# Keys, queries and the MLP's first matrix in 512-column products, a reordered second block, and 17 weight slots for the experts

## The chip, the cores and the metric

One core of one Trainium2 chip runs the whole program. The metric is the device time of one execution in microseconds (us). The core has TensorE (PE, with its weight loads, PEld, shown apart), VectorE (DVE), ScalarE (ACT), GpSimd (POOL) and SyncE (SP), which issues nearly all weight transfers. PSUM has eight banks of 128 x 512 float32.

## The reference, cut to what matters

Two layers of a first block, then one second block, on 256 tokens of width 1024, all in float32:

```
for l in (0, 1):
    x = x + rms(mixers(rms(x) @ w_in[l]) @ w_mix_out[l])           # NSA, retention, RWKV, conv
    q = rms(x) @ wq ; k, v = split(rms(mem) @ wkv)                  # cross attention, 4 heads of 256
    x = x + rms(softmax(q k^T / 16) v @ wo)
    x = x + rms(square(relu(rms(x) @ w1)) @ w2)                     # w1: 1024 x 4096
h = rms(x)                                                          # second block
x = x + groupnorm([attention, lru, convolution](h @ w_in_2)) @ w_out_2
x = x + sum over the 2 chosen of 32 experts of gate * (silu(h @ gate_e) * (h @ up_e)) @ down_e
```

## The kernel before, in words

The weights lie in DRAM as one stream of units of 128 x 2048 float32 (1 MiB each; `pieces` gives their order, `pack_weights` fills it). SP loads them in order (`load`, L2800) into ring slots; each load waits until its slot is free. Outside the experts and the convolution's taps, every unit is split in two float32r parts: ACT copies it rounded (`upper`, "hi"), DVE subtracts ("lo", L204, 128x2048). Both run LOOK = 2 units ahead, in `unit()`, which each engine's program calls once per unit; a split waits for PE to finish the unit three before. A product of two split operands is three products, high by high, high by low and low by high (`mm3`).

`proj` (L619) makes two 128 x 256 outputs of a unit: for each output eight k-steps of three 256-column products, 48 in all, into one bank. MLP: `up(g)` is two such units (L1040), `down(g)` two units of 24 products of 512 columns, 48 in all; PE runs up(g+1), then down(g). The accumulators of down hold four banks. ACT evicts up's result with Relu, DVE squares, ACT and DVE split it again. Keys and queries are eight `proj` units per layer with one ACT copy each.

`fill` spreads the units of the gates over the mixers' small products. In the retention and RWKV part of each layer ACT waits for `rsq`, takes the inverse root ("rvar"), and then does two fills; DVE does a fill after `aP`, another after `rout`, the lower part of oT1, then the masked matrices that PE's U, T and `within(3)` products wait for.

Second block: PE's program (from L1135) runs projections (bq, bk, cvl, cgt, vv, zx, xg), four tap units (float32 products with raw weights), log-space sums, and 26 filler products (`warm`, ones by constants) in three places; then three group norms and `tok_out(axv, "bout")`, which begins when all three norms are in both parts.

Experts (`few`, the path that these inputs take): six units each, four for gate and up, two for down, never split. There are SLOTS = 15 slots: 4 ring, 2 in ht, 6 in hl, 3 in the arena. Those 15 are loaded before the branch on the flag; after it every load waits for the unit that held its slot. Per expert PE does gate_up (2 x 16 products of 128x512, two 64-column tiles side by side), turn, place, scatter(e-1), gather, down (16). All of X stays in SBUF; four banks collect the expert outputs; at the end DVE adds them to X in four steps and ACT's queue stores two halves. A scatter is four float32 products with 64 rows.

## Time and profile before

| | |
|---|---|
| median of 3 runs | 1917.17 us (1914.98 to 1918.26) |
| the profiled execution | 1916.08 us, its span 1914.3 us, mean granted clock 0.994 |
| PE busy | 1850.7 us, 97% |
| DVE, ACT busy | 939.1 us (49%), 767.8 us (40%) |
| chain that ended last | 85% PE, 7% DVE, 3% ACT, 2% DMA |

A row of the timeline has its start, its length, engine, line, operation, tiles, shapes and count, and in brackets how long the engine sat idle before it and who ended that. A row of a windows table has the busy time of each engine in the stretch, the granted clock (1.00 is 2.4 GHz, 0.50 is 1.2 GHz), the DMA engines' share and GB/s.

### The profile page before, as it was taken

To read this page: it belongs to the slowest core of one execution; us is meant where nothing else is said; L and a number is where in the kernel's file an instruction comes from. 1 tells how busy PE (TensorE), PEld (TensorE's weight loads), DVE (VectorE), ACT (ScalarE), POOL (GpSimd) and SP (SyncE) were. 2 spreads that over 40 slices of the span, in tenths; PEclk is the share of its full clock that TensorE was granted. 3 is DMA by queue.
4 is the path that set the end of the run, shared out by engine and by line. 5 is a ranking of instruction groups with operands and counts; after the bars stand their busy time and mean duration, and the time that the engine had idled before them with its cause. 6 is when DMAs were issued, how large, how long until landed. Compare 5 with 4: busy or idle time off the path is not lost.

```text
span 1914.3 us, 28059 instructions
## 1 busy us (share of the span) xinstructions
PE 1850.7 (97%) x12114; PEld 1467.8 (77%) x12114; DVE 939.1 (49%) x1135; ACT 767.8 (40%) x1078; POOL 72.8 (4%) x90
## 2 busy tenths in 40 slices
PE   7998999999999999899999999999999999999998
PEld 6998998988999899899898899988874444444332
DVE  4866638646555686653864655575751111110001
ACT  4653344555444465334455544446532111111111
POOL 0000014000000000001400000000000000000000
PEclk9999999999999999999999999999999999999999
DMA  8434365534555533436553555543457999999996
GB/s 314 149 123 159 111 254 203 201 129 160 193 183 191 189 134 118 156 112 256 201 203 127 183 184 193 181 165 111 169 209 300 422 421 421 421 421 421 421 421 280
DMA packets 64512, 440.68 MB, mean 230 GB/s; under 512 B 7372, under 2 KB 7372, under 8 KB 14720
## 3 DMA queue, kind: packets, MB, share of 16 engines
q1 hardware_dynamic: 55296, 399.63, 54.4%
q0 software_dynamic: 8096, 35.30, 5.0%
q10 hardware_dynamic: 992, 3.90, 0.5%
q8 instruction: 97, 1.59, 0.3%
q14 instruction: 31, 0.25, 0.0%
HBM read 428.58 MB, written 10.23 MB: 229 GB/s over the span
## 4 chain that ended last, share of the span: by engine, by line
PE 85%; DVE 7%; ACT 3%; DMA 2%; POOL 2%; issue 1%; DVEq 0%; ACTq 0%; POOLq 0%
PE psum L190 83%; PE psum L194 2%; DVE arena L204 2%; DVE hl L204 2%; DVE arena L214 2%; POOL arena L204 1%; DMA ring<-W 1%; ACT arena L200 1%; ACT L200 1%; DMA cst<-CS 1%; ACT hl L200 0%; DVE ht L204 0%; ACT arena L201 0%; DVE arena L224 0%; DVE arena L227 0%
## 5 line engine op out<-in xcount | busy, mean ns | idle before, releaser
L190 PE MATMUL psum<-ht,hl 128*128 128x256 f32 x4992 | 622.5, 286 | 7.8 <-DVE ht L204 6.4
L190 PEld LDWEIGHTS psum<-ht,hl 128*128 128x128 f32 x4992 | 607.8, 193 | 18.6 <-DVE ht L204 7.7
L204 DVE TENSOR_TENSOR hl<-ring,hl 128x2048 fp32r<-128x2048 f32 (+1 forms) x188 | 428.7, 2286 | 308.9 <-ACT hl L200 308.5
L200 ACT ACTIVATE hl<-ring 128x2048 fp32r<-128x2048 f32 (+1 forms) x188 | 353.3, 1884 | 111.9 <-PE psum L190 102.4
L200 ACT ACTIVATE arena<-psum 128x512 f32<-128x512 f32 (+4 forms) x260 | 132.2, 509 | 391.9 <-PE psum L190 355.9
L190 PE MATMUL psum<-hl,ax 128*128 128x512 f32 x1056 | 243.7, 390 | 0.0
L190 PEld LDWEIGHTS psum<-hl,ax 128*128 128x128 f32 x1056 | 197.3, 188 | 40.2
L190 PE MATMUL psum<-arena 128*128 128x128 f32 (+8 forms) x1520 | 167.9, 290 | 9.9 <-DVE arena L204 7.4
L190 PEld LDWEIGHTS psum<-arena 128*128 128x128 f32 (+3 forms) x1520 | 152.8, 177 | 21.6 <-DVE arena L204 8.0
L204 DVE TENSOR_TENSOR hx_raw<-hx_raw,psum 64x512 f32<-64x512 f32 x32 | 22.1, 691 | 226.1 <-ACT hx_raw L200 226.1
L190 PE MATMUL psum<-hl,ht 128*128 128x512 f32 (+2 forms) x624 | 124.0, 358 | 1.1 <-DVE ht L214 1.1
L190 PEld LDWEIGHTS psum<-hl,ht 128*128 128x128 f32 x624 | 103.4, 189 | 19.5 <-DVE ht L214 1.9
L204 DVE TENSOR_TENSOR arena<-arena 128x512 f32<-128x512 f32 (+9 forms) x128 | 85.8, 670 | 42.2 <-ACT arena L200 36.0
L221 DVE COPY par<-psum 128x256 f32<-128x256 f32 x32 | 13.6, 424 | 185.2 <-PE psum L194 185.2
L190 PE MATMUL psum<-ax,hl 128*128 128x256 f32 x768 | 94.1, 284 | 0.0
L190 PEld LDWEIGHTS psum<-ax,hl 128*128 128x128 f32 x768 | 92.8, 192 | 1.1 <-issue 1.0
L190 PE MATMUL psum<-hl_raw,ax_raw 128*64 128x512 f32 x400 | 90.7, 596 | 0.0
L190 PE MATMUL psum<-cst 128*128 128x256 f32 x272 | 66.2, 401 | 15.7 <-DMA cst<-CS 12.5
L190 PE MATMUL psum<-ring,ax_raw 128*64 128x512 f32 x272 | 72.3, 595 | 0.8 <-DMA ring<-W 0.8
L190 PEld LDWEIGHTS psum<-cst 128*128 128x128 f32 x272 | 54.3, 203 | 23.5 <-DMA cst<-CS 12.5
L190 PE MATMUL psum<-hl_raw,par 128*64 128x512 f32 x224 | 72.1, 593 | 0.0
L201 ACT ACTIVATE arena<-psum 128x2 f32<-128x2 f32 (+1 forms) x56 | 19.9, 355 | 130.1 <-PE psum L190 129.3
(110 smaller groups left out, 1509.1 us busy)
## 6 DMA issues: line engine op xcount, KB each, us to landing
ring<-W SPq DMA_DIRECT2D x238, 1024.0 KB, 4.9
hl_raw<-W SPq DMA_DIRECT2D x78, 1024.0 KB, 17.8
arena<-W SPq DMA_DIRECT2D x36, 1024.0 KB, 17.1
ht_raw<-W SPq DMA_DIRECT2D x26, 1024.0 KB, 16.3
gate_d<-arena POOLq DMA_DIRECT2D x32, 256.0 KB, 3.9
arena<-gate_d POOLq DMA_DIRECT2D x8, 1024.0 KB, 8.9
gn<-GB POOLq DMA_DIRECT2D x10, 512.0 KB, 4.4
arena<-GB POOLq DMA_DIRECT2D x6, 512.0 KB, 5.1
```

The lines of the kernel that those rows point to most:

```text
L190: return Nothing() if self.e is None else self.e.matmul(o, a, b, start=start, stop=stop, skip_group_check=skip_group_check)
L194: return Nothing() if self.e is None else self.e.transpose(o, a, ident)
L200: return self.e.activation(o, a, f, bias=bias, scale=scale)
L201: return self.e.activation(o, a, f, bias=bias, scale=scale, accum_out=accum_out)
L204: return Nothing() if self.e is None else self.e.tensor_tensor(o, a, b, op)
L214: return Nothing() if self.e is None else self.e.scalar_tensor_tensor(out=o, in0=a, scalar=s, in1=b, op0=op0, op1=op1)
L221: return Nothing() if self.e is None else self.e.tensor_copy(o, a)
```

## The change

Four things, in one diff:

1. `proj_two` for keys, queries and up: high and low part of the activations stand behind each other as one 512-column operand under the high weights; the low weights meet the high part in a 256-column product. Two products per k-step, one bank per output (two per unit). ACT copies the second half of the bank, DVE adds the first (`met`).
2. Retention: ACT splits one unit before it waits for `rsq`, and DVE splits it before `aP`; DVE's fill and oT1's lower part move behind the masked matrices.
3. Second block: another order of units and of the three engines' steps; `xg` near the end with the group norm of attention between its halves; the first half of w_out starts when that norm alone is there; 6 fillers for 26.
4. Experts: X goes into the four accumulator banks by an identity product (in place of 9 fillers), its memory and that of `hf` become slots 16 and 17, loaded right behind the branch; the scatter takes high and low part of the output in one 128-row float32r product (ACT makes the high part, DVE the low); the last turn lies inside down(30); the results are copied out by ACT and DVE and stored from two queues.

```diff
+            def proj_two(rhs, *name):
+                u, wh, wl = unit()
+                both = (ht if rhs is hTv else ax)[:, :].rearrange("p (s k t) -> p k s t", s=2, k=8)
+                for q in range(2):
+                    b = bank(*name, q)
+                    cs = slice(128 * q, 128 * q + 128)
+                    for k in range(8):
+                        pe.matmul(psum[:, b, :], wh[:, k, cs], both[:, k, :, :], k == 0, False)
+                        ins = pe.matmul(psum[:, b, 0:256], wl[:, k, cs], both[:, k, 0, :], False, k == 7)
+                    ins.then_inc(s_pe, P(*name, q))
...
-                        pe.wait_ge(s_act, A["qx", 3, l])
+                        pe.wait_ge(s_dve, V["qx", 3, l])
...
                 fill()
+                unit()
                 ac.wait_ge(s_dve, V["rsq", l])
                 inverse_root(L.rrb, "eps5", 1.0 / 64, "rvar", l)
-                fill(2)
+                fill(begun=True)
+                fill()
...
+                def part(dst, *name):
+                    for q in range(2):
+                        ac.wait_ge(s_pe, P[(*name, q)])
+                        act(dst[:, q, :], half(banks[(*name, q)], 1), ACT.Copy, *name, "part", q, after=False)
...
+                def met(dst, *name):
+                    for q in range(2):
+                        ve.wait_ge(s_act, A[(*name, "part", q)])
+                        tt(dst[:, q, :], half(banks[(*name, q)], 0), dst[:, q, :], ADD, *name, after=False)
+                        gone(*name, q)
...
-                        tt(L.sq, L.rl, L.rl, MUL, "sq", g, i, l)
+                        met(L.rl, "up", g, i, l)
+                        stt(L.sq, L.rl, 0.0, L.rl, MAX, MUL, "sq", g, i, l)
...
-                fill()
-                ve.wait_ge(s_act, A["oT1", l])
-                lower(oT[1], L.rcen, "oT", 1, l)
+                fill(begun=True)
...
+            weighted(3)
+            proj(hTv, "xg", between=lambda: group_norm(0, 4, b2.zq[:, 0:4, :]))
...
-            warm(4)
-            group_norm(2, 2, ct1)
-            warm(10)
-            pe.wait_ge(s_dve, V["ynorm", 0])
+            warm(6)
...
+            for j in range(2):
+                u, _, _ = unit()
+                pe.wait_ge(s_dve, V["ynorm", 0])
+                for t in range(2):
+                    out_part(u, j, 0, t)
+                P.mark("unit", u)
+                if j == 0:
+                    group_norm(2, 2, ct1)
+                    group_norm(1, 2, b2.rec[3])
...
-            warm(9)
+            for t in range(2):
+                for j in range(2):
+                    b = bank("xacc", t, j, keep=True)
+                    ins = pe.matmul(psum[:, b, :], C("ident"), Xv[:, t, 512 * j:512 * j + 512], True, False, True)
...
-                            js = slice(64 * j, 64 * j + 64)
-                            ins = pe.matmul(psum[:, 2 * t + j, :], mo.SE[e % 3][js, t, :], mo.YE[e % 2][js, :], e == 0, e == 31)
+                            ins = pe.matmul(psum[:, banks["xacc", t, j], :], mo.SE[e % 3][:, t, :],
+                                            mo.YE[e % 2][:, 512 * j:512 * j + 512], False, e == 31, True)
...
+                elif m == 15:
+                    sp.wait_ge(s_pe, P["xacc"])
+                    sp.wait_ge(s_act, A["hf", 1])
+                elif m == 16:
+                    sp.wait_ge(s_pe, P["logits"])
```

On DVE the second block's last steps now run: attention's norm and its lower part, the recurrence, the convolution's output, the gelu product, then two `unit()` (two splits), the norms of group 2 and group 1.

## Rows read from the trace of the kernel before

**Rows 1.** The page: busy share of PE, and DMA share in 40 slices.
```profile
PE 1850.7 (97%) x12114; PEld 1467.8 (77%) x12114; DVE 939.1 (49%) x1135; ACT 767.8 (40%) x1078; POOL 72.8 (4%) x90
DMA  8434365534555533436553555543457999999996
```
**Rows 2.** Timeline of layer 0's MLP: down, up, down on PE; ACT evicts.
```profile
504.00 11.07 PE L190 MATMUL psum<-hl,ax 128*128 128x512 f32 x48
514.90 11.68 PE L190 MATMUL psum<-ht,hl 128*128 128x256 f32 x96
520.86 0.60 ACT L200 ACTIVATE arena<-psum 128x512 f32<-128x512 f32 x1 [3.78 <-PE psum L190]
526.42 3.82 PE L190 MATMUL psum<-hl,ax 128*128 128x512 f32 x16
```
**Rows 3.** Timeline behind the last query unit of layer 0, PE.
```profile
388.94 7.17 PE L190 MATMUL psum<-arena 128*128 128x256 f32 x32 [0.69 <-ACT arena L200]
```
**Rows 4.** Timeline of layer 0's retention and RWKV part.
```profile
137.95 3.70 ACT L200 ACTIVATE hl<-ring 128x2048 fp32r<-128x2048 f32 x2
139.88 2.29 DVE L204 TENSOR_TENSOR hl<-ring,hl 128x2048 fp32r<-128x2048 f32 x1 [5.15 <-ACT hl L200]
...
152.73 2.28 DVE L204 TENSOR_TENSOR hl<-ring,hl 128x2048 fp32r<-128x2048 f32 x1
158.11 2.08 PE L190 MATMUL psum<-arena 64*128 64x128 f32 x16 [3.64 <-DVE arena L204]
160.12 7.43 PE L190 MATMUL psum<-ht,hl 128*128 128x256 f32 x48
```
**Rows 5.** Windows: PE, PEld, DVE, ACT, POOL busy (count), PEclk, DMA share, GB/s.
```profile
158.00:160.00 2.00, 1.89 (x16) 1.78 (x16) 1.83 (x4) 0.00 (x0) 0.00 (x0) 0.50 0.57 242
```
**Rows 6.** Timeline of the second block before the experts.
```profile
1329.04 3.79 PE L190 MATMUL psum<-arena,cst 128*128 128x256 f32 x24 [3.23 <-DVE arena L214]
...
1383.08 5.34 PE L190 MATMUL psum<-cst 128*128 128x256 f32 x24
...
1389.26 1.75 DVE L227 RECIPROCAL arena<-arena 128x256 f32<-128x256 f32 x1
...
1395.08 1.58 PE L190 MATMUL psum<-arena,cst 128*128 128x256 f32 x4 [2.07 <-DVE arena L204]
1396.45 5.74 PE L190 MATMUL psum<-cst 128*128 128x256 f32 x20
...
1401.84 22.14 PE L190 MATMUL psum<-hl,ax 128*128 128x512 f32 x96
```
**Rows 7.** Windows of the expert stage: its start, its body, the last transfers.
```profile
1440.00:1453.00 13.00, 12.57 (x69) 9.36 (x70) 3.19 (x10) 2.82 (x7) 0.00 (x0) 0.87 0.03 10
1460.00:1880.00 420.00, 419.97 (x2102) 169.84 (x2100) 41.36 (x83) 69.18 (x175) 0.00 (x0) 1.00 1.01 421
1894.00:1900.00 6.00, 5.19 (x28) 2.44 (x28) 1.11 (x2) 1.28 (x2) 0.00 (x0) 1.00 0.30 126
```
**Rows 8.** The chain that ended last, in order of time: two experts' starts.
```profile
1473.89 13.62 PE psum L190 x66
...
1488.28 13.62 PE psum L190 x66
```
**Rows 9.** Timeline: a scatter inside the stage, and the end of the kernel.
```profile
1488.32 1.99 PE L190 MATMUL psum<-gn,arena 64*128 64x512 f32 x8
...
1894.92 0.69 DVE L204 TENSOR_TENSOR hx_raw<-hx_raw,psum 64x512 f32<-64x512 f32 x1 [6.19 <-ACT hx_raw L200]
...
1900.88 3.65 PE L190 MATMUL psum<-hl_raw,par 128*64 128x512 f32 x16
...
1904.58 0.69 ACT L200 ACTIVATE gn<-psum,arena 128x512 f32<-128x512 f32 x1 [5.92 <-PE psum L190]
1905.32 1.99 PE L190 MATMUL psum<-gn,arena 64*128 64x512 f32 x8 [0.79 <-ACT gn L200]
1906.49 2.48 DVE L204 TENSOR_TENSOR resid<-resid,psum 128x512 f32<-128x512 f32 x4 [6.86 <-PE psum L190]
```

More of the change, by code:

```diff
@@ L1186, in tensor @@
             ins.then_inc(s_pe, P("cpw"))
-            warm(4)
-            group_norm(2, 2, ct1)
-            warm(10)
-            pe.wait_ge(s_dve, V["ynorm", 0])
+            warm(6)
+            for t in range(2):
+                for j in range(2):
+                    bank("bout", t, j, keep=True)
+            for j in range(2):
[3 more added lines that the diff above has]
+                    out_part(u, j, 0, t)
+                P.mark("unit", u)
+                if j == 0:
+                    group_norm(2, 2, ct1)
+                    group_norm(1, 2, b2.rec[3])
+            two = [unit()[0] for _ in range(2)]
             pe.wait_ge(s_dve, V["ynorm", 1])
             pe.wait_ge(s_dve, V["ynorm", 2])
-            tok_out(axv, "bout")
+            for t in range(2):
+                for j in range(2):
+                    out_part(two[j], j, 1, t)
+                    if t:
+                        P.mark("unit", two[j])
+                    turn.give(banks["bout", t, j])
             P.mark("b2 end")
@@ L1316, in few @@
                         gather(g, i, shared)
-                    if e < 31:
-                        gate_up(e + 1, 1)
+                    gate_up(e + 1, 1)
                     if g < 8:
                         pe.wait_ge(s_act, A["x", g, i])
-                    down(e)
+                    down(e, between=last if e == 30 else None)
+                down(31)
+                scatter(30)
                 scatter(31)
             def many():
+                for t in range(2):
+                    for j in range(2):
+                        turn.give(banks["xacc", t, j])
                 def expert_in(e):
@@ L1670, in scalar @@
                     unit()
-                    ac.wait_ge(s_pe, P["qx", g, l])
-                    copy(L.qx[:, 2 * g:2 * g + 2, :], half(banks["qx", g, l]), "qx", g, l)
-                    gone("qx", g, l)
+                    part(L.qx[:, 2 * g:2 * g + 2, :], "qx", g, l)
                 for t in range(2):
@@ L1819, in scalar @@
             unit()
+            unit()
+            weights(0)
+            weights(1)
             ac.wait_ge(s_pe, P["zx"])
@@ L1822, in scalar @@
             gone("zx")
-            ac.wait_ge(s_dve, V["sm0"])
-            act(sm[:, :, 1:2], sm[:, :, 0:1], ACT.Exp, "lam exp")
-            act(sm[:, :, 2:3], sm[:, :, 1:2], ACT.Ln, "lam", bias=C("ones")[:, 0:1])
-            weights(0)
-            weights(1)
-            unit()
-            ac.wait_ge(s_pe, P["xg"])
-            copy(b2.xg, half(banks["xg",]), "xg")
-            gone("xg")
+            unit()
+            take_ya(0)
+            take_ya(1)
+            keeps(3)
+            unit()
+            weights(2)
             for nm, dst, o in (("wa", t1, 0), ("wx", t2, 2)):
@@ L1855, in scalar @@
             gone("cu")
-            group_root(1, 2, aL)
-            take_ya(3)
+            unit()
+            weights(3)
+            ac.wait_ge(s_dve, V["loga"])
+            act(aL, t1, ACT.Exp, "aL")
             ac.wait_ge(s_pe, P["cvar"])
@@ L1860, in scalar @@
             gone("cvar")
-            group_root(0, 4, b2.zq[:, 4:6, :])
-            group_cut(1, 2)
+            take_ya(2)
+            take_ya(3)
+            act(t3, t1, ACT.Tanh, "t3")
             ac.wait_ge(s_dve, V["cnorm"])
             act(ct1, cu, ACT.Tanh, "csilu", scale=0.5)
+            group_root(0, 4, b2.zq[:, 4:6, :])
+            ac.wait_ge(s_dve, V["uvar"])
+            act(t1, t1, ACT.Sqrt, "ustd", scale=-1.0)
+            ac.wait_ge(s_pe, P["xg"])
+            copy(b2.xg, half(banks["xg",]), "xg")
+            gone("xg")
             group_cut(0, 4)
+            ac.wait_ge(s_dve, V["gelu"])
+            act(t3, t3, ACT.Tanh, "gelu", scale=math.sqrt(2.0 / math.pi))
+            unit()
+            unit()
             group_root(2, 2, ct2)
+            group_root(1, 2, aL)
             group_cut(2, 2)
-            for _ in range(3):
+            group_cut(1, 2)
+            for _ in range(2):
                 unit()
@@ L2264, in vector @@
                     masked(1, i)
+                fill()
+                ve.wait_ge(s_act, A["oT1", l])
+                lower(oT[1], L.rcen, "oT", 1, l)
                 fill()
@@ L2649, in few @@
             def few():
-                shared = 6
                 def prep(g):
```

339 lines of the change are left out of this document (201 added, 138 removed).

## The prediction

> **What bounds the kernel now.** I read the page first. PE is busy for 97% of the span and the DMA engines reach nine tenths only in the last quarter [rows 1]. So up to about 1440 us the time is PE's, and a step there is worth what it takes from PE, or from a wait of PE. Then I read PE's timeline in three places. In the MLP products follow each other without a gap [rows 2]. In the retention part PE waits for DVE [rows 4], and the granted clock falls to 0.50 (1.2 GHz) behind that wait [rows 5]. In the second block fillers and waits alternate [rows 6]. The windows and the chain give the expert stage: PE takes 14.39 us per expert [rows 8], while 421 GB/s bring an expert's six units of 1.049 MB in 14.95 us [rows 7]. PE is the faster of the two and lives on the 15 stocked units; the stock runs out just at the end. The transfers stood still from 1440 to about 1453 [rows 7], because all slots were full.
>
> **The change part by part.** The sum is made against the profiled execution, 1916.08 us (span 1914.3 and 1.8 around it), 1.1 us under the median of 1917.17.
>
> *512-column products.* 96 products of 256 columns take 526.42 - 514.90 = 11.52 us, 120.0 ns each; 48 of 512 columns take 514.90 - 504.00 = 10.90 us, 227.1 ns each [rows 2]. A k-step is 3 x 120.0 = 360.0 ns now and 227.1 + 120.0 = 347.1 ns then, 12.9 ns less. There are 48 units (per layer 4 keys, 4 queries, 16 up) of 16 k-steps, 768: 9.9 us. No row shows the split operand (two stretches of 256 columns) or the alternation of widths. If weight loads cost the 120 ns, a k-step could stay at 360 (gain 0) or, if the 256-column product shrinks behind a long one to 227.1/2 = 113.6 ns, save 19.3 ns (14.8 us). I take 9.9, since both terms are measured in this stage.
>
> The Trainium skill (TensorE: Matmul & The Clock Gate, Back-to-back issue gap) puts a warm product at its columns over 2.4 GHz plus 2.5 ns; by it the fixed part that a k-step saves would be 2.5 ns and the whole 1.9 us in place of 9.9. The rows disagree with it: 120.0 and 227.1 ns leave over 13 ns per product, so the sum stays with the rows.
>
> The new work lies beside PE. ACT copies two halves instead of one bank (0.60 us for 512 columns [rows 2]) and DVE gains two additions of 256 columns per unit, under 0.69 us each (a 512-wide step on half the partitions, [rows 9]). With split (2.29), square and lower part that is under 5.1 us on DVE per up unit, against 5.5 us of PE and another 10.9 us of down for every two. Banks: up now takes two of the four that down leaves, and gets a bank back after two units; the eviction ends about 3.2 us behind the unit and PE asks 5.5 us behind it. Without that cover each late bank would cost its lateness 32 times. In front of the scores PE now waits for ACT and DVE in turn instead of ACT alone (idle 0.69 us [rows 3]): +0.3 us per layer, +0.6. Sum of this part: -9.3; bounds +1 and -14.
>
> *Retention.* PE sat 3.64 us before 158.11 waiting for a bank that DVE frees with its second T step [rows 4]; three more waits before it make 6.7 us, and at 0.50 the next 48 products took 7.43 us in place of 6.0. DVE's queue in between holds three splits of 2.29, and the first waited for ACT, which came to it only at 137.95 behind the inverse root. The change puts that split before `aP`, so the masked matrices start about 4 us earlier. But they are followed by both remaining splits, and the second of these now waits for ACT, which makes its high part only behind oT1's lower part. By hand: masked matrices end at 145.4, split 147.7, oT1 148.4, ACT's copy 150.3, split 152.7, T steps 155.6, against 158.1. That is 2.5 us per layer and 5.0 for two; the clock still falls. Bounds: 0, and 9 per layer if the waits and the slow clock all go. I take 5.0.
>
> *Second block.* From 1268.07 (its first product) to 1401.84 PE spends 133.8 us. In it are 26 fillers, 12 of them in 5.34 us and the last ten in 5.74, 12.9 in all, and five waits, the first 3.23, the last 2.07, together 8.8 [rows 6]. Work: 112.1 us. The new order has six fillers (2.7 us). Placing the three engines' steps I find three waits, for `cu` (1.1), `cusq` (1.7) and the square of attention's output (2.2): 5.0. The first half of w_out (48 products, 10.9 us) then ends at 1268.1 + 112.1 + 2.7 + 5.0 + 10.9 = 1398.8. The second half needs the other two norms. On DVE they stand behind the recurrence and the gelu product (ends about 1392.7), then two splits (4.6), and for each norm a reciprocal of 1.75 [rows 6], two products of 0.5, a wait for ACT's rounding and a lower part of 0.69: about 1405.6. So PE waits near 6 us and the clock falls as it does in rows 5, worth 2.5. End: 1405.6 + 10.9 + 2.5 = 1419.0, against 1401.84 + 22.14 = 1424.0. Gain 5.0; bounds -16 (no wait) and +3 (two waits more of this size). The SP loads behind these units keep their distance to the end of w_out, so the stage behind it only moves.
>
> *Experts.* The stock grows from 15 to 17 units. Both loads fit in the 13 us in which nothing moved, and their slots are empty by then; so 175 units instead of 177 come after 1453, at 1.049 MB / 421 GB/s = 2.49 us each: -5.0. The scatter falls from 1.99 us [rows 9] to four products of 227 ns, so PE would need 13.4 us per expert; being still faster than the transfers, it gains nothing. The identity products (four float32 ones of 512 columns, about 3.4 us) take the place of nine fillers (4.0): 0. DVE's two extra steps per expert (0.69 each, ACT first) end under 3 us behind down, beside gate_up's 3.65. The tail: the last units land near 1898.5 [rows 7]; now down(31) starts at 1900.88, since turn(31), scatter(30) and its weights come in turn [rows 9]. In the new order turn(31) is done by then, and down starts as its weights land: -2.4. Behind it the output needs two ACT and one late DVE step (1.9 in place of 0.69), scatter 0.9 for 2.0, copies on two engines 1.2 for 2.5, hence about -1.2 more, and scatter(30), 0.9, lies now in the cover of the former: together -2.7. Sum -7.7; bounds -3 and -12.
>
> Sum: -9.3 - 5.0 - 5.0 - 7.7 = -27.0; 1916.1 - 27.0 = 1889.1, or 1890.2 by the median. I predict 1890.
>
> **The rivals.**
> *A k-step that stays at 360 ns.* For it: 256-column products are 13 ns over their columns, and nobody knows whether that is the load of weights. Against: the 512-column ones are over by the same. The gain is then 27.0 - 9.9 = 17.1: 1900.
> *The second block without its last wait.* For it: my DVE time is a hand schedule, and a split or two may have run earlier. Against: the order in the diff puts both before the norms. Another -8: 1882.
> *The experts turn from DMA to PE (slower).* PE now waits for transfers 1.6 us per expert once the stock is used up, by my numbers from about expert 18 on. Waits of 2 to 4 us were followed by 0.50 in rows 5 and behind 1395.08 [rows 6]. If that happens here, 13.4 us of work become up to 26.8 against 14.95 of supply. PE decides below a mean clock of 13.4 / 14.95 = 0.90. At 0.75 an expert costs 17.9, 2.9 more, 14 times 41 us: 1931. Against it: single waits would be under 1.4 us, and a late PE finds its stock full and has no waits. [...] No row of this stage shows a clock below 1.00 between 1460 and 1880 [rows 7], but there PE had no waits.
> *The change doesn't do what it says:* the two slots are loaded too late to be of use and the banks of up make PE wait. Then only retention, block and tail remain, about 1905.
>
> **How the numbers follow.** Forecast, all four terms near their values (1884 to 1896): 0.55. K-step at 360: 0.12. No last wait: 0.17. Late slots or banks: 0.09. PE-bound experts: 0.04. Other: 0.03. The range leaves out the slow rival, 1905 and a little below 1882: 1879 to 1902. The likeliest is 1890. About 0.2% (4 us) is what a measurement here can tell from no change. Faster by more: 0.94; within: 0.02; slower: 0.04.
>
> **What would show it.** MLP: 96 products of up (now 64) in about 11.1 us instead of 11.52, and no idle PE before them. Retention: the wait before `within(3)` at 155 to 156 less the earlier shift. Second block: a wait of about 6 us before the last 48 products of w_out, the end of w_out 5 us nearer to the block's first product. Experts: 421 GB/s throughout, two loads within 2 us of the branch, PE idle 1.6 us per expert in the last third, the last transfer 5 us nearer to the branch. The prediction is wrong if PE waits for banks in up, if the clock in the last third is under 0.9, or if transfers pause after 1455.

## The result and the profile after

The changed kernel takes 1896.53 us (median; 1893.93 to 1898.58) against 1917.72 (1914.98 to 1918.53): a ratio of 0.9889, 95% interval 0.9875 to 0.9903, that is 21.2 us less. I had predicted 1890.0, 27.0 less, with a range of 1879 to 1902. The profiled execution took 1893.93 us with a span of 1892.0, 22.3 less than before. The direction and three of the four terms came out near their values; the largest term came out at a third.

The page of the changed kernel: busy time, then the DMA engines' share and GB/s in 40 slices.

```profile
PE 1805.5 (95%) x11168; PEld 1416.6 (75%) x11168; DVE 1020.0 (54%) x1293; ACT 795.9 (42%) x1157; POOL 72.9 (4%) x90
DMA  8444365534555434336553455442458999999997
```

PE is busy for 95% of the span where it was 97% [rows 1], with 946 records of products fewer, and DVE has 81 us more to do.

To see where the time went I used DVE's 188 splits (128x2048) as milestones, since the n-th split is the same step in each kernel, outside the retention part and the second block. Each column is the length of a stretch of the run: start to split 13; retention and RWKV of layer 0 (to split 21); from there to the MLP (split 57: the gates, output product, keys, queries); MLP (93); the same of layer 1 with its retention (109, 145, 181); the second block to the branch (PE's 12 fillers behind it); branch to the first gate product on DVE; from there to the 32nd; the tail. The first line has us in the changed kernel's profile, each other line what a profile has more or less than that.

```
               start  ret.0  keys0   MLP0  ret.1  keys1   MLP1  block branch experts  tail    sum
changed       100.19  68.69 288.11 202.99 137.56 277.63 214.70 137.29  15.94  431.00 17.94 1892.04
before         -0.03  +2.96  -0.51  +1.76  +2.67  +0.64  +1.46  +4.31  +1.43   +6.11 +1.43  +22.25
predicted              +2.5   +1.4   +3.3   +2.5   +1.4   +3.3   +5.0     (  +5.0  ) +2.7   +27.0
```

The lines of after that answer to [rows 2] and [rows 3]: PE in layer 0's MLP (down, up, down) and the start of the scores.

```profile
478.73 11.11 PE L191 MATMUL psum<-hl,ax 128*128 128x512 f32 x48
489.68 11.45 PE L191 MATMUL psum<-ht,hl 128*128 128x512 f32 x64
500.96 11.11 PE L191 MATMUL psum<-hl,ax 128*128 128x512 f32 x48
...
386.52 1.78 PE L191 MATMUL psum<-arena 128*128 128x256 f32 x7 [0.93 <-DVE arena L205]
```

The 64 products of up follow each other without idle time (so no wait for banks in up, as predicted) and take 500.96 - 489.68 = 11.28 us, where 96 took 11.52. That is 352.5 ns for a k-step: a gain of 7.5 ns, not 12.9. Down takes 10.95 where it took 10.90.

The keys of layer 0, with DVE's step that held them up:

```profile
333.40 0.69 DVE L205 TENSOR_TENSOR arena<-psum,arena 128x512 f32<-128x512 f32 x1 [2.03 <-DMA arena<-GB]
...
337.36 5.80 PE L191 MATMUL psum<-ax,hl 128*128 128x512 f32 x32
344.67 5.89 PE L191 MATMUL psum<-ax,hl 128*128 128x512 f32 x32 [1.51 <-DVE resid L215]
```

Between two key units stands a wait that the kernel before didn't have: there the 96 products of these two units are one piece.

```profile
340.28 11.68 PE L190 MATMUL psum<-ax,hl 128*128 128x256 f32 x96
```

The second unit now takes two banks, and its banks were those of the mixers' output, which DVE gave back only after it had added them to X. DVE had itself stood for 2.03 us for a gain vector. In layer 1 the same wait is 0.50. From the first key product to the first of the scores it is 49.16 us in layer 0 (386.52 - 337.36) and 48.16 in layer 1; before, it was 48.66 in both (388.94 - 340.28 in layer 0). So in keys and queries one layer lost half a us and the other gained it.

Retention, layer 0, after ([rows 4, 5] before): PE, DVE, ACT, then the window behind the wait.

```profile
156.07 2.08 PE L191 MATMUL psum<-arena 64*128 64x128 f32 x16 [5.07 <-DVE arena L205]
158.08 6.54 PE L191 MATMUL psum<-ht,hl 128*128 128x256 f32 x48
...
150.68 2.29 DVE L205 TENSOR_TENSOR hl<-ring,hl 128x2048 fp32r<-128x2048 f32 x1 [1.98 <-ACT hl L201]
153.07 0.69 DVE L205 TENSOR_TENSOR arena<-psum,cst 128x512 f32<-128x512 f32 x1
...
155.32 0.69 DVE L205 TENSOR_TENSOR arena<-psum,cst 128x512 f32<-128x512 f32 x1
...
148.73 1.91 ACT L201 ACTIVATE hl<-ring 128x2048 fp32r<-128x2048 f32 x1 [7.46 <-DVE ax L205]
...
156.00:158.00 2.00, 1.93 (x16) 1.79 (x16) 1.83 (x4) 0.00 (x0) 0.00 (x0) 0.50 0.54 225
158.00:160.00 2.00, 2.00 (x13) 1.92 (x12) 1.83 (x4) 0.00 (x0) 0.00 (x0) 0.68 0.00 0
```

within(3) starts at 156.07 where it started at 158.11: my hand schedule said 155.6. Its wait is now one of 5.07 in place of four that came to 6.7, and it ends with DVE's second T step, which stands behind a split, which stands behind ACT, which sat 7.46 us waiting for oT1's lower part.

Second block, after ([rows 6] before): PE, then DVE.

```profile
1383.65 1.89 PE L191 MATMUL psum<-arena,cst 128*128 128x256 f32 x8
1385.20 5.83 PE L191 MATMUL psum<-hl,ax 128*128 128x512 f32 x24
1397.27 13.24 PE L191 MATMUL psum<-hl,ax 128*128 128x512 f32 x48 [6.24 <-DVE ax L205]
...
1384.13 4.49 DVE L205 TENSOR_TENSOR hl<-ring,hl 128x2048 fp32r<-128x2048 f32 x2
1388.72 1.75 DVE L228 RECIPROCAL arena<-arena 128x256 f32<-128x256 f32 x1
...
1392.94 1.75 DVE L228 RECIPROCAL arena<-arena 128x256 f32<-128x256 f32 x1
```

The wait of 6 us before the last 48 products is there (6.24), and they take 13.24 us instead of 10.9, 2.3 more. From the block's first product (1259.11) to the last of w_out (1410.5) it is 151.4 us; predicted 150.9, before 155.9.

Experts: windows of their first and last part, PE's first wait for weights, then pieces of the chain that ended last, with the tail at its end ([rows 7, 8, 9] before).

```profile
1460.00:1660.00 200.00, 199.47 (x1020) 87.39 (x1019) 44.96 (x76) 47.67 (x106) 0.00 (x0) 1.00 1.01 421
1680.00:1860.00 180.00, 161.33 (x798) 69.79 (x798) 34.94 (x57) 37.20 (x82) 0.00 (x0) 1.00 1.01 421
...
1655.08 0.61 PE L191 MATMUL psum<-resid,ax_raw 128*64 128x512 f32 x1 [0.54 <-DMA arena<-W]
...
1472.50 12.54 PE psum L191 x62
...
1485.80 12.54 PE psum L191 x62
...
1626.94 27.93 DMA arena<-W
...
1879.11 3.67 PE psum L191 x16
1883.52 0.74 DVE rounded L215
```

PE needs 13.30 us per expert (1485.80 - 1472.50), the transfers run at 421 GB/s throughout, and the chain changes from PE to DMA with the transfer that starts at 1626.94. PE first waits for weights at 1655.08, before the first product of the 18th expert. Between 1680 and 1860 PE is idle for 18.7 of 180 us, 1.6 per expert, and the clock stays at 1.00.

### The profile page after: what moved, and what is told of

Same layout as the page of the kernel before. It is cut to its first block, busy times and chain, and to the rows that moved or that the text cites. A ratio compares the mean times of both kernels' runs of the same rounds, so it can differ in the third digit from the quotient of the medians.

```text
span 1892.0 us, 26308 instructions
## 1 busy us (share of the span) xinstructions
PE 1805.5 (95%) x11168; PEld 1416.6 (75%) x11168; DVE 1020.0 (54%) x1293; ACT 795.9 (42%) x1157; POOL 72.9 (4%) x90
## 4 chain that ended last, share of the span: by engine, by line
PE 73%; DMA 13%; DVE 8%; ACT 3%; POOL 2%; issue 1%; DVEq 0%; ACTq 0%; POOLq 0%
PE psum L191 71%; DMA hl_raw<-W 5%; DMA arena<-W 3%; DVE arena L205 2%; PE psum L195 2%; DVE hl L205 2%; DMA resid<-W 2%; DMA ring<-W 2%; DVE arena L215 2%; POOL arena L205 1%; DMA ht_raw<-W 1%; ACT arena L201 1%; ACT hl L201 1%; ACT L201 1%; DMA cst<-CS 1%
## 5 line engine op out<-in xcount | busy, mean ns | idle before, releaser
L191 PE MATMUL psum<-ht,hl 128*128 128x256 f32 (+1 forms) x4352 | 616.3, 302 | 7.1 <-DVE ht L205 6.6
L191 PEld LDWEIGHTS psum<-ht,hl 128*128 128x128 f32 x4352 | 570.7, 191 | 46.8 <-DVE ht L205 8.0
L201 ACT ACTIVATE arena<-psum 128x256 f32<-128x256 f32 (+5 forms) x278 | 128.9, 466 | 373.4 <-PE psum L191 339.8
L215 DVE SCALAR_TENSOR_TENSOR rounded<-psum,arena,rounded 64x512 fp32r<-64x512 f32 x64 | 48.0, 750 | 94.9 <-ACT rounded L201 93.9
L191 PE MATMUL psum<-ax,hl 128*128 128x256 f32 (+1 forms) x640 | 93.2, 306 | 2.0 <-DVE resid L215 2.0
L205 DVE TENSOR_TENSOR arena<-psum,arena 128x256 f32<-128x256 f32 (+2 forms) x141 | 66.6, 490 | 40.8 <-ACT arena L201 29.2
L191 PE MATMUL psum<-arena,ax_raw 128*64 128x512 f32 x240 | 80.0, 597 | 5.3 <-DMA arena<-W 2.6
L191 PE MATMUL psum<-ring,ax_raw 128*64 128x512 f32 x240 | 79.9, 596 | 5.3 <-DMA ring<-W 2.6
L201 ACT ACTIVATE rounded<-psum,arena 64x512 fp32r<-64x512 f32 x64 | 43.7, 682 | 97.3 <-PE psum L191 96.5
L191 PE MATMUL psum<-rounded 128*128 128x256 f32 (+2 forms) x448 | 76.0, 315 | 1.2 <-DVE rounded L215 1.2
```

Source lines behind the costliest of these rows:

```text
L191: return Nothing() if self.e is None else self.e.matmul(o, a, b, start=start, stop=stop, skip_group_check=skip_group_check)
L201: return self.e.activation(o, a, f, bias=bias, scale=scale)
L205: return Nothing() if self.e is None else self.e.tensor_tensor(o, a, b, op)
L215: return Nothing() if self.e is None else self.e.scalar_tensor_tensor(out=o, in0=a, scalar=s, in1=b, op0=op0, op1=op1)
```

## Experiments

Each kernel was timed beside the kernel before on the same chip. The four a kernels shared one chip, b1, b2, b3 and b5 another, and b4 and the c kernels a third.

```
                         median us (lowest to highest)   ratio to before, 95% interval
a1 narrow products       1901.17 (1899.40 to 1908.24)    0.9914 (0.9894 to 0.9934)
a2 old retention         1899.65 (1898.84 to 1902.63)    0.9897 (0.9879 to 0.9914)
a3 old second block      1903.87 (1902.36 to 1909.51)    0.9917 (0.9901 to 0.9933)
a4 15 slots              1900.80 (1899.00 to 1906.67)    0.9900 (0.9882 to 0.9919)
b1 wide, then narrow     1894.67 (1892.61 to 1902.70)    0.9876 (0.9858 to 0.9895)
b2 cut by norm           1892.51 (1890.28 to 1895.10)    0.9867 (0.9846 to 0.9888)
b3 T steps first         1887.79 (1884.75 to 1888.98)    0.9839 (0.9819 to 0.9858)
b5 banks given earlier   1899.26 (1893.75 to 1904.04)    0.9912 (0.9885 to 0.9939)
c0 changed kernel        1896.90 (1894.45 to 1898.17)    0.9883 (0.9862 to 0.9904)
b4 more work for PE      1923.39 (1919.83 to 1925.80)    1.0026 (1.0015 to 1.0037)
c1 four edits            1876.24 (1875.28 to 1880.03)    0.9782 (0.9763 to 0.9802)
c2 and fillers           1872.37 (1871.42 to 1880.91)    0.9778 (0.9752 to 0.9803)
```

Intervals of 0.4% are as wide as most single terms, so a term is read from the same stretches of the profiles (more or less than the changed kernel's):

```
               start  ret.0  keys0   MLP0  ret.1  keys1   MLP1  block branch experts  tail    sum
c0             -0.01  +1.34  -0.17  -0.46  +1.01  +1.15  +0.04  +0.09  -0.01   +1.08 +0.18   +4.24
a1             +0.13  +0.48  -0.50  +1.56  -0.20  +0.53  +1.46  +0.95  +0.00   -0.38 +0.01   +4.04
a2             +2.44  +2.09  -0.12  -0.05  +1.74  -0.37  -0.02  -0.01  -0.01   -0.10 +0.38   +5.97
a3             +8.56  +0.10  -0.16  -0.01  +0.10  -0.07  +0.00  +5.48  +1.63   -0.15 +0.18  +15.67
a4             +6.00  +1.30  -0.20  -0.02  +0.83  -0.08  +0.06  +0.93  -0.01   +3.95 -0.02  +12.74
b1             +8.05  +0.32  +0.29  -1.38  +0.66  +0.17  -1.33  +1.01  +1.41   -0.32 -0.01   +8.86
b2             +0.01  +0.23  -0.39  -0.46  +0.49  +0.00  +0.00  -2.08  +1.68   +0.67 -0.03   +0.11
b3             +2.19  -5.72  -0.29  -0.05  -6.06  +1.41  -0.11  +0.90  +1.66   +1.10 +0.02   -4.95
b5             -0.01  +0.37  -1.73  -0.01  +0.98  +0.51  +0.02  +0.80  +0.00   -0.98 -0.03   -0.09
b4             +0.16  +0.46  -0.06  -0.05  +0.31  +0.00  +0.02  +0.90  +1.66  +24.99 +1.78  +30.17
c1             -0.16  -5.72  -0.10  -1.39  -6.08  -0.89  -1.48  -1.70  +0.01   -0.13 +0.19  -17.46
c2             -0.06  -5.73  -2.18  -1.39  -6.09  -0.89  -1.49  -4.70  +0.00   +0.67 -0.04  -21.89
```

c0 is the changed kernel once more, and its line is the yardstick: an MLP repeats to 0.5 us, but a stretch with a wait of several us in it only to 1 or 1.3, since the slow clock behind the wait is not equally long each time. The window that was at 0.68 above is at 0.50 in c0, and the 48 products in it took 7.86 us instead of 6.54:

```profile
158.00:160.00 2.00, 2.00 (x11) 1.91 (x10) 1.83 (x4) 0.00 (x0) 0.00 (x0) 0.50 0.00 0
```

The start varies by up to 8.6 us from one execution to the next, whatever the kernel, so single spans are no measure of an edit here. Some other stretches can be judged in the profiles whose kernels have the same steps there. With the retention's order of the change (nine profiles) they average 0.5 us more than the first line in each layer; the block with the new order (nine) reaches up to 1.0 more; the expert stretch with 17 slots and this PE work (eleven) runs from 0.98 less to 1.10 more.

**a1: keys, queries and up in 256-column products.**

```diff
-                        proj_two(hTv, "up", g, i, l)
+                        proj(hTv, "up", g, i, l)
...
-                part(L.rl, "up", g, i, l)
+                act(L.rl, half(banks["up", g, i, l]), ACT.Relu, "up", g, i, l)
```

> The changed kernel (1896.5 us) with keys, queries and up back in 256-column products (three per k-step, one bank per unit, one copy by ACT); all else as changed. My sum gave this part 9.3 us (k-step 360.0 to 347.1 ns, less 0.6 for two waits): 1905.8. The rival reads the trace of the changed kernel: its k-steps in up take 352.8 ns and those of keys and queries between 346.6 and 353, and 2 us of new waits for banks stand among the keys (1.51 of them in layer 0); 16 x 8 x 2 + 8 x 16 k-steps per layer give 3.3 us, less 2.6 of waits in all: 4.0, so 1900.5. If the products don't matter at all it stays at 1896.5. The second block and the expert stage keep their lengths in all three.

Measured 0.9914 against 0.9889 and 0.9883 of the changed kernel, and in the profile 1.56 - 0.50 + 0.53 + 1.46 = 3.05 us more in keys and MLPs. The ratio says more than that, 4.8 to 5.9 us, but 1.6 of it isn't in the products: in all six runs of a1 the time is 3.3 to 3.7 us over the span of its instructions, in every other kernel's runs 1.7 to 2.0. Why is open. The pairs bring 3 us in the MLPs and nothing in the keys and queries: from the first key product to the scores a1 takes 48.65 us in each layer, the changed kernel 49.16 and 48.16. My 9.3 is refuted; the rival (4.0) is near.

**a2: the old order of the retention part.**

```diff
                 fill()
-                unit()
                 ac.wait_ge(s_dve, V["rsq", l])
                 inverse_root(L.rrb, "eps5", 1.0 / 64, "rvar", l)
-                fill(begun=True)
-                fill()
+                fill(2)
```

> The changed kernel with the retention part's old order on ACT and DVE (split behind aP, lower part of oT1 ahead of the masked matrices). My sum gave this order 2.5 us per layer, 5.0 in all: 1901.5, with the wait before within(3) about 1.4 us shorter than the 5.07 of the changed kernel and within(3) 2.5 us later. The rival: the trace shows 2.04 us at within(3) and 2.93 behind the fill after it (a fill at full clock gains 0.9 more), so 5.9: 1902.4. If what is gained there is lost again at the next wait of the same layer, the time stays near 1896.5 and the products after the gates start at the same time.

In the profile 2.09 and 1.74, 3.8 us; by the ratios 1.5 to 2.7 us; before against after 2.96 and 2.67, 5.6. My 5.0 lies inside, but of these numbers up to 1.3 us per layer is the length of the slow clock (c0's line), which the new order doesn't control. The changed kernel's own profile is at the short end of it in layer 0; against the average of the nine profiles with this order, the kernel before takes 4.7 us more in both layers and a2 2.9.

**a3: the old second block**, with its units' order and its 26 fillers. The edit is the second block's part of the diff, taken back in PE's, ACT's and DVE's program and in the weights' order.

```diff
-            warm(6)
+            warm(12)
...
+            warm(4)
+            group_norm(2, 2, ct1)
+            warm(10)
```

> The changed kernel with the second block's old order of units and of the three engines' steps and its 26 fillers; pairs, retention and experts as changed. My sum gave the new order 5.0 us: 1901.5, from the block's first product to the last of w_out 155.9 us. The trace shows 4.3: 1900.8. A third way: the new order pays also behind the block, since the first half of w_out no longer stands before the branch alone and its loads come sooner; then over 1903.

5.48 us more in the block; predicted 5.0. The 1.63 behind the branch isn't the block's: five of the other profiles show 1.4 to 1.7 there, the kernel before among them, with the clock at 0.50 for part of it, in the others it is 0.

**a4: without the two slots.**

```diff
-        free = [X[:, 0:UNIT], arena[:, ar["n"]:ar["n"] + UNIT]]
+        free = []
```

> The changed kernel without the two slots in X and hf: after the branch every load waits for a unit that has been used, as in the kernel before. My sum gave the two slots 5.0 us (two units at 2.49 us less behind the pause): 1901.5, the last transfer about 5 us later behind the branch, 421 GB/s and a clock of 1.00 as before. The rival, that the loads are late or the supply isn't what ends the stage: 1896.5. If PE's idle time had cost clock, the version with less idle time would be the faster one: under 1896.5.

3.95 us more between the first and the last expert, predicted 5.0; since this stretch repeats only to about 1 us, 5.0 is unlikely but not excluded. It also tells how the rest of the stage came about: with 15 slots and the new scatter this stretch takes 434.95 us, before it took 437.11. So about 2.2 us came from PE's shorter work per expert, which I had put at nothing; this too rests on one profile each.

**b1: 512-column products first, then the 256-column ones.**

```diff
                     for k in range(8):
                         pe.matmul(psum[:, b, :], wh[:, k, cs], both[:, k, :, :], k == 0, False)
+                    for k in range(8):
                         ins = pe.matmul(psum[:, b, 0:256], wl[:, k, cs], both[:, k, 0, :], False, k == 7)
```

> The changed kernel, but within a bank all eight 512-column products come first and then the eight 256-column ones, instead of one of each in turn. Theory one, the alternation of widths costs: k-steps of up go from 352.8 to 227.1 + 120.0 = 347.1 ns, as I predicted for them; 16 units x 16 x 5.7 ns per layer and 0.2 for the first two key units, 3.3 us in all: 1893.2. Theory two, the pace is set by something else of the stage (its banks, the copies of ACT and DVE beside it): 352.8 ns stay and so does 1896.5. Theory three, two weight loads in a row from the low part cost more than loads that alternate: slower.

PE in b1's MLP:

```profile
586.25 11.31 PE L191 MATMUL psum<-ht,hl 128*128 128x512 f32 x64
597.40 11.07 PE L191 MATMUL psum<-hl,ax 128*128 128x512 f32 x48
```

up takes 597.40 - 586.25 = 11.15 us, 348.4 ns a k-step, and each MLP is 1.3 to 1.4 us shorter. So theory one: the two widths in turn cost what I had missed. The single starts inside the changed kernel's up repeat in threes, 233 + 117, 241 + 120, 236 + 113 ns (353.3 on average). Among the queries the same pair of products runs at 231 + 113 and 232 + 118 and comes to 346.6, just what I had predicted. It isn't the place in the program that decides. The first 128 products of layer 0's MLP, in the changed kernel's profile and in that of c0, the same program:

```profile
456.02 22.88 PE L191 MATMUL psum<-ht,hl 128*128 128x512 f32 x128 [1.50 <-DVE ht L205]
```

```profile
457.18 22.46 PE L191 MATMUL psum<-ht,hl 128*128 128x512 f32 x128 [1.50 <-DVE ht L205]
```

From the ninth k-step to the last the one runs at 353.3 and the other at 346.6. A run of such pairs has two steady rhythms and keeps the one it falls into at its start: in the nine profiles with such pairs in up, every up that stands behind down, in both layers, is at 353.2 to 353.4, and every run from the third key unit to the last query at 346.6 to 346.7. What picks it stays open. Wide products in a row, 226.7 ns each, and narrow ones in a row, 120.0, don't have the slow one; only the first five wide ones behind narrow ones take up to 236 ns, which is why b1's k-step is 348.4 and not 346.7.

**b2: the last quarter of w_out cut by norm.**

```diff
-            pe.wait_ge(s_dve, V["ynorm", 1])
             pe.wait_ge(s_dve, V["ynorm", 2])
             for t in range(2):
                 for j in range(2):
-                    out_part(two[j], j, 1, t)
+                    out_part(two[j], j, 1, t, (2, 3), False)
+            pe.wait_ge(s_dve, V["ynorm", 1])
+            for t in range(2):
+                for j in range(2):
+                    out_part(two[j], j, 1, t, (0, 1))
```

> The changed kernel, with the second half of w_out cut by norm: first the 24 products of group 2 (convolution), whose norm is done at 1392.9, then the 24 of group 1 (recurrence), done at 1397.1. Theory one, the last wait is DVE's time alone: the 6.24 us before the last 48 products fall to about 1.9, 24 products fill the time until 1398.4, no second wait of over 0.5, and since PE stands still for less the granted clock stays at 1.00: end of w_out 6 us earlier, 1890.5. Theory two, the clock falls all the same: 24 products cost 2.5 us more, and the gain is 3 to 4: 1893. Theory three, the end of the block is set by the norm behind it (two halves of tokens on ACT and DVE), so that the stage's end doesn't follow: under 2 us.

PE in b2: the end of the block.

```profile
1394.18 12.76 PE L191 MATMUL psum<-hl,ax 128*128 128x512 f32 x48 [2.02 <-DVE ax L205]
1407.20 1.32 PE L195 MATMUL psum<-cst,arena 128*128 128x128 f32 x8 [0.26 <-DVE arena L215]
```

The wait falls from 6.24 to 2.02 and no second one comes, but the products still take 12.76 us, 1.9 over full speed, as in theory two. The products behind w_out start 3.15 us earlier (1410.35 in the changed kernel), inside its 3 to 4; at the branch 2.1 of them are left.

**b3: the T steps ahead of the second split, and ACT's high part ahead of its wait.**

```diff
+                unit()


                 ac.wait_ge(s_dve, V["oT", 1, l])
-                fill()
+                fill(begun=True)
...
                 ve.wait_ge(s_act, A["oT1", l])
                 lower(oT[1], L.rcen, "oT", 1, l)
-                fill()
                 one = C("ident").unsqueeze(1).broadcast_to([128, 4, 128])
                 for c in range(2):
...
                     level(1, c)
+                fill()
```

> The changed kernel; in the retention part DVE makes the two T steps before its second split instead of behind it, and ACT makes the high part of that split before it waits for the lower part of oT1. Theory one, within(3) waits for the bank that the second T step frees and for nothing else: that step ends at 151.7 instead of 156.0, within(3) starts at about 151.9 after at most 1 us of waiting, and the products behind the next fill 4.5 us earlier; 9 us for two layers: 1887.5. Theory two, what is gained is lost at the next steps because DVE has the same work in all and is the engine that sets the pace: within(3) earlier, the first U step not: 1896.5. Between them: 2 us per layer, 1892.5, if the next fill waits for the split that has been put back.

PE in b3, layer 0 (this execution's steps are 2.19 us late from its start on):

```profile
153.98 1.16 PE L191 MATMUL psum<-arena 64*128 64x128 f32 x16 [0.79 <-DVE arena L205]
155.07 6.02 PE L191 MATMUL psum<-ht,hl 128*128 128x256 f32 x48
...
154.00:156.00 2.00, 2.00 (x23) 1.88 (x24) 1.97 (x3) 1.39 (x1) 0.00 (x0) 1.00 0.49 201
```

The wait of 5.07 is one of 0.79, the clock stays at 1.00, and so 16 + 48 products that took 2.0 + 6.4 us take 1.1 + 5.9. The two stretches are 5.72 and 6.06 us shorter, more than the 4.5 each of theory one, and the median is 1887.79 (1887.5 by theory one). Later stretches of the profile are longer (+1.41, +0.90, +1.66, +1.10); in each of these four the clock stood at 0.50 once more than in the changed kernel's profile. In the change's own order more than half of what the retention part had to give was still left.

**b5: banks given back at the first reading.**

```diff
                     tt(tmp[:, js], psum[:, banks[(*name, t, j)], :], gb[:, js], MUL, after=j == 0)
+                    gone(*name, t, j)
...
                     stt(Xv[:, t, js], tmp[:, js], rs[:, 6 + t:7 + t], Xv[:, t, js], MUL, ADD, *name, "x", t, j, after=j == 0)
-                    gone(*name, t, j)
...
-                gain(f"xa{l}")
                 post(L.gb, 7 * l)
+                gain(f"xa{l}")
```

> The changed kernel; behind the mixers' output DVE tells that a bank is free as soon as it has read it (two steps earlier), and GpSimd loads the post gain before the other one. Theory one, the second half of the keys' gain was lost to banks (1.51 us before the second key unit in layer 0, 0.5 in layer 1, DVE being held 2.0 us by the gain's transfer before): waits of 0.3 at most, 1.7 us less: 1894.8. Theory two, the wait only moves to the norm between the key units, which needs the same DVE steps: 1896.5.

PE in b5: both key units in one piece, no wait; then the scores.

```profile
337.72 11.45 PE L191 MATMUL psum<-ax,hl 128*128 128x512 f32 x64
...
385.14 7.17 PE L191 MATMUL psum<-arena 128*128 128x256 f32 x32 [0.93 <-DVE arena L205]
```

Layer 0's keys stretch is 1.73 shorter, as theory one has it; layer 1's is 0.51 longer, within c0's scatter for it (1.15). The time from the first key product to the scores leaves that scatter out: 47.42 us in both layers, 1.74 and 0.74 less than in the changed kernel. So theory one holds in both layers, and without the waits the pairs bring 1.24 us per layer in keys and queries. The medians don't tell b5 from the changed kernel.

**b4: more work for PE in the experts.**

```diff
                     pe.wait_ge(s_dve, V["aT", e])
+                    for k in range(2):
+                        for j, (_, w) in enumerate(two):
+                            pe.matmul(psum[64 * j:64 * j + 64, result(e), :], mo.aT[e % 2][:, k, :], w[:, k, :], k == 0, k == 1)
                     for k in range(4):
```

> The changed kernel with four more products per expert on PE (the first quarter of down's products twice; the result is the same), 4 x 0.228 = 0.9 us per expert, 29 us of PE in all; PE's pace is then 14.2 us per expert as in the kernel before. Theory one, the transfers end the stage (421 GB/s, 14.95 us per expert): at most 1 us slower, 1897, PE idle less in the last third. Theory two, PE ends it: 29 us slower, 1925. Theory three, the idle time of PE costs clock and filling it gains: under 1896.

I had mis-sized the dose: a product in full float32 is two records of the trace (the 16 of one half of gate and up, or of down, are eight products), so four of them are 1.72 us, and PE's pace is 15.02 us per expert, just above the transfers' 14.9. Windows of b4 at the end:

```profile
1860.00:1880.00 20.00, 20.00 (x99) 7.26 (x96) 3.73 (x6) 3.93 (x9) 0.00 (x0) 1.00 1.01 420
1884.00:1920.00 36.00, 30.99 (x145) 11.41 (x144) 8.01 (x12) 7.01 (x13) 0.00 (x0) 0.98 0.08 29
```

The last weights land at 1883.3, counted from the first gate product within 1 us of the changed kernel's, and the program goes on for 39 us behind them, in the changed kernel for 13: 25.0 us more for the stretch. So it is no test of the old pace by itself, but it shows the account that I had missed: PE ends the stage not from 14.95 on, but from the pace at which its work takes as long as the transfers with the stock taken off.

**c1 and c2: the four edits together, and fillers.** c1 is b1 (in up and the first two key units), b2, b3 and b5. c2 adds one line:

```diff
+            warm(4)
             pe.wait_ge(s_dve, V["ynorm", 2])
```

> The changed kernel itself, for comparison on the same chip: 0.9889 of the kernel before as measured; by its trace the layers end 8.96 us earlier, the second block gives 4.3 more and the expert stage 9.0.

> The changed kernel with four edits: 512-column products first in up and in the first two key units; last quarter of w_out cut by norm; T steps ahead of the second split; banks freed at their first reading. If the gains that the traces of the single edits show add up (2.8, 2.2 at the branch, 10.8 and 1.4), it is 17.2 us below the changed kernel: 1879.3. If the 2.2 and part of the others are lost at the pause of the transfers behind the branch, where the third load waits for the first used unit, 1882. If an edit gains only because another wait was there to hide in, less: over 1884.

> The kernel with the four edits and, on top, four filler products (1.8 us) in the 2.0 us in which PE waits for the norm of group 2. Theory one, standing still is what lowers the granted clock to 0.50 at 1395 (3.4 us of it, worth 1.7): with the fillers the clock stays and the end of w_out comes 1.7 us earlier than without them. Theory two, the clock falls anyway there, or falls elsewhere: no difference. Theory three, the fillers end behind the norm: up to 0.5 slower.

c1 takes 1876.24 us, 20.7 less than c0 beside it and 0.9782 of the kernel before; its profile has 17.5 us less than the changed kernel's, expected 17.2. PE in c1 and in c2 before the end of w_out:

```profile
1377.21 12.78 PE L191 MATMUL psum<-hl,ax 128*128 128x512 f32 x48 [2.04 <-DVE ax L205]
```

```profile
1373.40 1.89 PE L191 MATMUL psum<-cst 128*128 128x256 f32 x8
1375.44 11.18 PE L191 MATMUL psum<-hl,ax 128*128 128x512 f32 x48 [0.16 <-DVE ax L205]
...
1376.00:1386.00 10.00, 10.00 (x45) 8.26 (x44) 4.53 (x8) 2.37 (x6) 0.00 (x0) 1.00 0.48 197
```

With the fillers the wait is 0.16, the clock stays at 1.00 and the 48 products take 11.18 us instead of 12.78: theory one, 1.6 us where 1.7 was expected. Counted from the block's start, w_out ends 1.4 us earlier. The block is 3.0 us shorter than c1's; the rest of that lies behind w_out, where the slow clock is shorter in c2's execution, and which I can't put down to the fillers. This is one profile against two (b2 and c1, both slow behind that wait), and theory two isn't wholly out: in c2 the clock had fallen once earlier in the block, at 1351.5, behind a wait of 1.93, where in c1 it hadn't. The median is 1872.37, but two of its five runs (1878.90, 1880.91) are above the median of c1 and one above its slowest, and the two intervals overlap, so the times don't show that c2 beats c1. Both beat the changed kernel clearly.

## Why the prediction was right, and where it was not

The time lies in the range, with about four fifths of the gain. Of the profile's 22.3 us, 1.4 are the clock behind the branch and no merit of the change.

*512-column products: predicted 9.3, measured 3.0 to 3.3.* The step that failed is "I take 9.9, since both terms are measured in this stage". 227.1 and 120.0 ns were measured among their own kind, and their sum held for the queries (346.6) but not in up, where the alternation costs another 6 ns. With 512 k-steps of up gaining 7.5 ns instead of 12.9, 2.8 us are missing there, and down gives 0.05 us back in each turn (0.8 us). I had named that nothing showed the alternation, and then didn't charge for it. The other part is the banks. I placed them for up, where PE indeed never waits, and not for the keys, where the units before had left theirs with DVE: waits of 1.51 + 0.50 us, which cost 1.74 + 0.74 us by b5. The three come to 6.1, and 9.3 less 6.1 is 3.2. a1 gives 3.05 for the whole term. Without the two waits the keys and queries would have given 2.5 us, near the 2.7 of my sum for them.

*The Trainium skill's rule* (TensorE: Matmul & The Clock Gate, Back-to-back issue gap), which that section gives for an isolated product and not for a stream with weight loads, would have made it 1.9 us. By its total it is nearer than my sum, but not by its reason: the rows give 226.7 ns for 512 columns and 120.0 for 256, 13 ns over the columns, against its 2.5.

*Retention: predicted 5.0, measured 5.6 between the two profiles, 3.8 in a2 (4.7 and 2.9 against the average of nine).* The hand schedule was right to 0.5 us: the masked matrices earlier, the second split behind ACT, the T steps at the end. What I put in as "the clock still falls" was right too, and b3 shows what it costs when it doesn't: my bound of 9 per layer was the place to look for the next gain.

*Second block: predicted 5.0, measured 4.3, and 5.5 in a3.* The wait near 6 us (6.24) and the 2.5 us of slow clock behind it (2.3) came as worked out. The rival without the last wait is refuted. The bound of -16 for that case doesn't come from the sum's own terms: 5.0 with the wait (1405.6 - 1398.8 = 6.8) and its 2.5 on top is 14.3.

*Experts: predicted 7.7, measured 7.5 (6.1 between the first and the last expert, 1.4 in the tail).* That it is so near is luck: three terms were off and their errors cancelled. The slots gave 3.95 by a4, not 5.0. And "being still faster than the transfers, it gains nothing" was wrong. Before, PE was hardly ever idle in this stage (419.97 of 420 us with records [rows 7], one wait of 0.77 at 1884): at 14.39 us per expert it had to work as long as the stage lasted, and the transfers ended at nearly the same time. The changed kernel's PE stands in waits for 21.9 of the 431.0 us. Spread over 31 experts that is 0.7 us each, and 13.30 + 0.7 = 14.0: up to about that pace the transfers end the stage, above it PE does. (An estimate; from the two profiles in which PE doesn't wait, 437.1 us at 14.39 and 456.0 at 15.02, the stretch would reach 431.0 at 14.2.) The old pace, 14.39, lies above both. So with the old scatter the two slots would have brought at most the 0.8 us that PE stood idle; that follows from these numbers and wasn't run by itself. a4 shows the other half: the faster scatter without slots is worth 2.2. The tail gave 1.4 of its 2.7. Another 1.4 stand behind the branch and aren't the change's: the clock fell there in the kernel before, and it did so too in b1 to b4, which have the changed kernel's steps there.

*The slow rival* (PE becomes the bound because its clock falls in the waits) is refuted. PE waits 1.6 us per expert as predicted, from the 18th expert on, where I had put it, in waits of up to 1.52 us, and the clock is 1.00 from 1460 to 1860. The Trainium skill (same page, HAM oscillation) tells of a loop in whose every turn the clock falls anew, with waits for DMA of about 3 to 5 us; the waits here are about half of that or less, and behind none of them does it fall. A longer one did come in b3's execution, and the clock fell behind it, once: the eight products (16 records) took 5.22 us in place of 3.65.

```profile
1680.40 5.22 PE L191 MATMUL psum<-hl_raw,ax_raw 128*64 128x512 f32 x16 [2.87 <-DMA hl_raw<-W]
...
1680.00:1684.00 4.00, 3.60 (x10) 1.29 (x12) 0.00 (x0) 0.00 (x0) 0.00 (x0) 0.57 1.01 422
```

Outside the experts, waits of 5.07, 2.02 and 6.24 us were followed by 0.50, waits of 0.79 and 0.16 weren't. In between it differs from one execution to the next, with the same steps: the wait of 2.2 us before the 12 fillers behind the block was followed by 0.50 in b1 to b4 and not in the changed kernel's two profiles, and two waits of 1.1 and 0.9 us, before layer 0's keys, were in c0 and not in the changed kernel's other profile.

## What to carry to other kernels

Where two engines end a stage nearly together, a shorter time for one of them is worth little alone (here 2.2 us for PE's, at most 0.8 for the transfers') and more together with the other (6.1), so each should be priced with the other at its new value. A product's duration measured in a run of its own kind is not its duration in turn with another kind; put equal ones behind one another and measure the pair. When an output is cut over more banks, ask who held the banks before, and give a bank back at its last reading rather than after the whole step. In this kernel a wait of 2 us and more cost its length and, in most places, the slow products behind it too: where a hole of 2 us was filled with four useless products, the products behind it took 1.6 us less, in the one profile taken. Before comparing two profiles, take the same kernel's a second time: a single stretch can differ by more than the term that is looked for.

## What the runs showed of the hardware

- The same pair of products (512 and 256 columns, a weight load before each) runs steadily at 346.6 or at 353.3 ns, and the same stage of the same program shows the one in one execution and the other in another (22.46 and 22.88 us for 128 products). With equal widths in a row the single products take 226.7 and 120.0 ns, and the first five wide ones behind narrow ones up to 236, 348.4 per k-step in all.
- The start of the program up to the 13th split took 100.0 to 108.8 us, though the kernels have the same instructions there.
- In the experts a 512-column product in full float32, side by side with another on the other half of the array's columns, costs 0.43 to 0.46 us (eight products, 16 records, 3.65 us; four more, 1.72).
- The same program's slow stretch behind the same wait of 5.07 us was longer in one execution than in another: the next 48 products took 6.54 and 7.86 us.
- In the experts 18 waits for weights of 0.5 to 1.5 us, one or two per expert, left the granted clock at 1.00; one of 2.87 us was followed by 0.50 (b3).
